# Branch A's last pair woven into the first gate product of a hybrid encoder layer, on one Trainium2 core

## The reference

```python
h = layer_norm(x, ln_in_g, ln_in_b)
proj = h @ w_in[l]
(aq, ak, av, ag, bq, bk, bv, bf, bg, cq, cg, mg) = split_columns(proj)
oa = swa_sink_attention(...)    # A: 16 query heads, 2 kv heads, window of 128, sinks, relative bias
ob = forgetting_attention(...)  # B: 16 heads, causal, cumulative forget bias
oc = memory_attention(...)      # C: 4 heads over 256 memory tokens
branches = (oa * silu(ag), ob * silu(bg), oc * silu(cg))
for n in range(3):
    gate = sigmoid(mg[..., n * D_MODEL:(n + 1) * D_MODEL] + b_gate[l, n])
    merged += gate * (branches[n] @ w_branch[l, n])
y = merged @ w_out[l]
h = layer_norm(alpha * h + y, ln_g[l], ln_b[l])
```

## Time and profile before

| | us |
|---|---|
| median of three runs | 1889.51 (1888.16 to 1889.75) |
| the profiled execution | 1889.29 |
| its span | 1887.7 |
| PE busy | 1852.6 (98% of the span) |
| DVE busy | 1221.1 (65%) |
| ACT busy | 829.6 (44%) |
| POOL busy | 162.1 (9%) |

### The profile page before, as it was taken

One profiled execution on the slowest core, in us unless ns is written; L12 is line 12 of the kernel. 1 busy time (PEld: TensorE's weight loads), 2 busy tenths in 40 slices (PEclk: granted clock), 3 DMA queues, 4 the chain that ended last, 5 costly groups with the idle time before them and its releaser, 6 DMA issues.

```text
span 1887.7 us, 24332 instructions
## 1 busy us (share of the span) xinstructions
PE 1852.6 (98%) x8599; PEld 1529.5 (81%) x8599; DVE 1221.1 (65%) x1909; ACT 829.6 (44%) x1360; POOL 162.1 (9%) x225
## 2 busy tenths in 40 slices
PE   8999999999999999999989999999999999999996
PEld 6888887888888888888878888888888888888884
DVE  5754335654555554677868878778788655576776
ACT  4652222544444444344445545455456333234543
POOL 1100000000000000000000000000001000002223
PEclk9999999999999999999999999999999999999998
DMA  8554446433333333333242623605437544439998
GB/s 306 189 153 127 128 134 205 117 86 96 102 91 91 88 90 95 98 98 103 85 162 71 212 85 139 223 23 200 144 124 247 200 155 145 147 115 242 242 210 193
DMA packets 227033, 271.95 MB, mean 144 GB/s; under 512 B 12768, under 2 KB 150032, under 8 KB 224784
## 3 DMA queue, kind: packets, MB, share of 16 engines
q1 hardware_dynamic: 196400, 188.24, 32.0%
q0 software_dynamic: 30416, 82.22, 16.3%
q10 hardware_dynamic: 144, 0.52, 0.1%
HBM read 229.38 MB, written 37.32 MB: 141 GB/s over the span
## 4 chain that ended last, share of the span: by engine, by line
PE 95%; DMA 2%; DVE 1%; POOL 1%; ACT 0%; issue 0%; DVEq 0%; POOLq 0%; SPq 0%; ACTq 0%
PE acc L634 13%; PE acc L636 13%; PE acc L635 13%; PE scores L958 4%; PE scores L956 4%; PE scores L954 4%; PE acc L954 3%; PE acc L958 3%; PE acc L956 3%; PE transposed L661 3%; PE scores L1024 2%; PE scores L1026 2%; PE scores L1025 2%; PE acc L1024 2%; PE acc L1026 2%; PE acc L1025 2%
## 5 line engine op out<-in xcount | busy, mean ns | idle before, releaser
L634 PE MATMUL acc<-h_hi,w_lo 128*128 128x512 f32 x1056 | 420.6, 398 | 0.0
L636 PE MATMUL acc<-h_hi,w_hi 128*128 128x512 f32 x1056 | 412.0, 390 | 0.0
L635 PE MATMUL acc<-h_lo,w_hi 128*128 128x512 f32 x1056 | 411.1, 389 | 0.0
L1557 DVE TENSOR_TENSOR w_lo<-raw_weights,w_hi 128x1024 fp32r<-128x1024 f32 x214 | 260.9, 1222 | 229.5 <-ACT w_hi L1106 224.0
L1106 ACT ACTIVATE w_hi<-raw_weights 128x1024 fp32r<-128x1024 f32 x214 | 225.8, 1058 | 277.9 <-PE acc L636 115.7
L1356 ACT ACTIVATE piece_split<-w 128x512 fp32r<-128x512 f32 x336 | 212.0, 632 | 221.5 <-PE acc L958 81.3
L2004 DVE TENSOR_TENSOR piece_split<-w,piece_split 128x512 fp32r<-128x512 f32 x336 | 231.9, 691 | 87.4 <-ACT piece_split L1356 78.5
L636 PEld LDWEIGHTS acc<-h_hi,w_hi 128*128 128x128 f32 x1056 | 198.2, 188 | 42.3
L634 PEld LDWEIGHTS acc<-h_hi,w_lo 128*128 128x128 f32 x1056 | 198.9, 188 | 41.1 <-issue 2.8
L635 PEld LDWEIGHTS acc<-h_lo,w_hi 128*128 128x128 f32 x1056 | 198.6, 188 | 39.7 <-issue 1.0
L954 PE MATMUL scores<-piece_split,h_sums 128*128 128x512 f32 x216 | 84.0, 389 | 0.0
(11 more groups left out here) (423 smaller groups left out, 3522.9 us busy)
## 6 DMA issues: line engine op xcount, KB each, us to landing
raw_weights<-in_w_in SPq DMA_DIRECT2D x134, 512.0 KB, 3.8
w<-in_w_in SPq DMA_DIRECT2D x96, 512.0 KB, 8.2
raw_weights<-in_w_branch SPq DMA_DIRECT2D x48, 512.0 KB, 5.2
raw_weights<-in_w_mem_kv SPq DMA_DIRECT2D x32, 512.0 KB, 5.2
gate<-gate_scratch POOLq DMA_DIRECT2D x12, 1024.0 KB, 6.6
gate_scratch<-first_product POOLq DMA_DIRECT2D x12, 512.0 KB, 6.7
out_w_x<-in_w_out POOLq DMA_DIRECT2D x12, 512.0 KB, 8.2
x_rows<-in_x SPq DMA_DIRECT2D x4, 1024.0 KB, 9.0
```

Of the source, the lines that this page charges most:

```text
L634: pe.matmul(bank_out, wl, hi[:, k, :], start=first, stop=False)
L635: pe.matmul(bank_out, wh, lo[:, k, :], start=False, stop=False)
L636: return pe.matmul(bank_out, wh, hi[:, k, :], start=False, stop=last)
L1557: dve.tensor_tensor(w_lo[:, slot, :], raw[:, slot, :], w_hi[:, slot, :].bitcast(F32), ALU.subtract).then_inc(lo_ready, 1)
```

## The change

1. **PE's order.** Of the last pair only turns 0 and 1 stay ahead of the gates. `gate_product` takes hooks: behind G1's piece 0 come turns 2 and 3, behind piece 1 the values stage.
2. **ACT and DVE.** Pieces 0 and 1 are split at the end of the last pass, ahead of the last tanh and silu, and so are turned tiles 0 and 1; tiles 2 and 3 follow the silu. `a_parts` stands behind piece 3. `a_gate` is cut into `a_join` (behind pieces 5 and 6) and `a_multiply` (behind piece 7).
3. **Banks.** In even groups G1 accumulates in `sc[0]`, `sc[1]` and G5 in `acc[0]`, `acc[1]`; in odd groups the third role changes likewise. G1 of the first group waits for the maxima of all scores (`a_negmax`), G5 for `acc_free`.
4. **Weight sums of the first group.** `first_sums` puts the first sums of pieces 0 to 3 behind the splits of pieces 4 to 7, and so on; the split of the tile `s3` (`h_lo`, second half of tokens) moves from G6 to G2.
5. **Loads.** `w_12` is loaded quarter by quarter, each as soon as the chunk that used its slot has been multiplied.
6. **Layout.** Branch A's probabilities and bias move down and its values and silu up, so that slots 0 and 1 of `p_split` are free in the last pass. The constants shrink by 160 bytes, and all of the region `R2` starts 160 bytes lower.

```diff
-    R2 = CONST + 3072
+    R2 = CONST + 2912
...
-                if g == 0:
-                    sp.wait_ge(multiplied, CH_M)
-                for d in range(4):
+                for n in range(CH_M - RING, CH_M):
+                    d = n % RING
                     if g:
                         sp.wait_ge(pc_lo, piece(g - 1, G7, 2 * d + 1) + 1)
+                    else:
+                        sp.wait_ge(multiplied, n + 1)
                     load_pieces(g, "12", w_12, 0, 1, d)
...
-            for t in range(TT):
-                a_turn_stage(PAIRS, t)
-            a_values_stage(PAIRS, 1)
-
+            a_turn_stage(PAIRS, 0)
+            a_turn_stage(PAIRS, 1)
+            a_end = {0: lambda: (a_turn_stage(PAIRS, 2), a_turn_stage(PAIRS, 3)),
+                     1: lambda: a_values_stage(PAIRS, 1)}
...
                     last.then_inc(pc_mult, 1)
+                    if between and k in between:
+                        between[k]()
...
-                a, b, c = (acc[0], acc[1]), (sc[0], sc[1]), (sc[2], ob)
+                a, b, c = (sc[0], sc[1]), (acc[0], acc[1]), (sc[2], ob)
                 z, y, x = (a, b, c) if g % 2 == 0 else (c, b, a)
+
+                if g == 0:
+                    pe.wait_ge(a_negmax, 2 * PAIRS)
+                else:
+                    pe.wait_ge(ev_c11, 2 * g)
+                gate_product(g, G1, z, True, False, a_end if g == 0 else None)
...
                     split_hi(CH_A + s, 4, i)
+                if at_end:
+                    at_end()
                 job_done(CH_A + 3, 4, i)
                 act.wait_ge(gated, 2 * BT + i)
                 tanh_half(JOB_A + 1, a_e[:, :])
...
-            piece_hi(0, G1, 0)
-            a_probs_hi(PAIRS, (0, 1, 2, 3))
-            act.wait_ge(a_o, PAIRS)
-            piece_hi(0, G1, 1)
-            a_parts(PAIRS)
+            def first_pieces():
+                piece_hi(0, G1, 0)
+                piece_hi(0, G1, 1)
+                a_probs_hi(PAIRS, (0, 1))
...
+            a_pass(PAIRS - 1, False, first_pieces)
+
+            a_probs_hi(PAIRS, (2, 3))
...
+                        if g == 0 and p == G1 and k == 3:
+                            a_parts(PAIRS)
...
                 a_normalise(i, steps)
+                if at_end:
+                    at_end()
                 silu(JOB_A + 1, 2, i, a_e[:, :], a_sg[:, :], 2 * HC + PAIRS + 1 + i, steps)
...
-            piece_lo(0, G1, 0)
-            a_probs_lo(PAIRS, (0, 1, 2, 3))
-            piece_lo(0, G1, 1)
-            a_gate(PAIRS)
-            dve.wait_ge(gated, 3 * BT)
+            def first_pieces():
+                piece_lo(0, G1, 0)
+                piece_lo(0, G1, 1)
+                a_probs_lo(PAIRS, (0, 1))
...
+            a_pass(PAIRS - 1, False, first_pieces)
             dve.sem_inc(ev_c12, 2)
-            dve.sem_inc(ev_c21, 2)
+            a_probs_lo(PAIRS, (2, 3))
...
+            first_sums = {at_pk: due for at_pk, due in sums_in.items() if at_pk[0] not in (G1, G5, G6)}
+            for k in range(4):
+                first_sums[G1, k + 4], first_sums[G5, k] = (1, k), (1, k + 4)
+                first_sums[G5, k + 4], first_sums[G6, k] = (2, k), (2, k + 4)
+                first_sums[G6, k + 4] = (3, k)
...
-                        if (p, k) in sums_in:
-                            weight_sum(g, *sums_in[p, k])
-                        if g == 0 and p == G6 and k == 4:
+                        if g == 0 and p == G1 and k in (5, 6):
+                            a_join(PAIRS, k - 5)
+                        if g == 0 and p == G1 and k == 7:
+                            a_multiply(PAIRS)
+                            dve.wait_ge(gated, 3 * BT)
+                            dve.sem_inc(ev_c21, 2)
+                        if (p, k) in (sums_in if g else first_sums):
+                            weight_sum(g, *(sums_in if g else first_sums)[p, k])
+                        if g == 0 and p == G2 and k == 2:
                             dve.wait_ge(s3_hi, 1)
```

More of the change, by code:

```diff
@@ L280, in program @@
     a_k = at(R2 + 2048, "a_k", [P, 2, SEQ], F32)
[L281 to L289, removed]
+    a_v = at(R2 + 16384, "a_v_hi_lo", [P, TT, 2, 2, 64], F32R)
+    a_sg = at(R2 + 20480, "a_silu", [P, SEQ], F32)
+    a_e = at(R2 + 22528, "a_tanh", [P, SEQ], F32)
+    a_bias = at(R2 + 6144, "a_bias", [P, 2, WIN], F32)
+    a_p = at(R2 + 8192, "a_probs", [P, TT, 2, 2 * P], F32)
+    a_sum = at(R2 + 24576, "a_attended", [P, TT, P], F32)
+    a_vt = at(R2 + 26624, "a_v_transposed", [P, SEQ], F32)
+    a_out = at(R2 + 26624, "a_gated", [P, SEQ], F32)
+    s3_buf = at(R2 + 28672, "s3_tile", [P, HALF], F32)
     a_pth = at(BR_HI, "a_probs_t_hi", [P, TT, 3 * P], F32R)
@@ L944, in _, with gate_product @@
                 left[p] = [h_sum[:, n, v, :, :] for v in range(2)]
-            def gate_product(g, p, banks, first, stop):
+            def gate_product(g, p, banks, first, stop, between=None):
                 hi, lo = left[p]
@@ L1303, in a_parts, with a_pass @@
                         .then_inc(a_part_ready, 1)
-            def a_pass(i, first):
+            def a_pass(i, first, at_end=None):
                 for s in range(4):
@@ L1867, in a_probs_lo, with a_join, a_multiply @@
                                       ALU.subtract).then_inc(copied, 1)
-            def a_gate(i):
-                for b in range(2):
-                    dve.wait_ge(a_part_ready, b + 1 - 2 + 2 * i)
-                    high = (ob, sc[2])[b][0:64, :].rearrange("p (t h q) -> p t h q", t=2, h=2)
-                    low = a_part[:, b, :].rearrange("p (t h q) -> p t h q", t=2, h=2)
-                    for hh in range(2):
-                        dve.tensor_tensor(a_sum[hh * 64:(hh + 1) * 64, 2 * b:2 * b + 2, :], high[:, :, hh, :],
-                                          low[:, :, hh, :], ALU.add).then_inc(a_summed, 1)
+            def a_join(i, b):
+                dve.wait_ge(a_part_ready, b + 1 - 2 + 2 * i)
+                high = (ob, sc[2])[b][0:64, :].rearrange("p (t h q) -> p t h q", t=2, h=2)
+                low = a_part[:, b, :].rearrange("p (t h q) -> p t h q", t=2, h=2)
+                for hh in range(2):
+                    dve.tensor_tensor(a_sum[hh * 64:(hh + 1) * 64, 2 * b:2 * b + 2, :], high[:, :, hh, :],
+                                      low[:, :, hh, :], ALU.add).then_inc(a_summed, 1)
+            def a_multiply(i):
                 dve.wait_ge(a_summed, 4 * i)
@@ L1983, in a_pass @@
                     if s == 1 and not first:
-                        a_gate(i)
+                        a_join(i, 0)
+                        a_join(i, 1)
+                        a_multiply(i)
                     if s == 2:
@@ L2040, in branch_lo @@
                                   ALU.subtract).then_inc(branch_ready, 1)
[L2042 to L2046 removed]
+            def first_pieces():
+                piece_lo(0, G1, 0)
+                piece_lo(0, G1, 1)
+                a_probs_lo(PAIRS, (0, 1))
+            dve.wait_ge(br_stored, 16 * (HC + PAIRS))
+            dve.wait_ge(toep_stored, 16 * PAIRS)
+            a_pass(0, True)
+            with dve.Fori(1, PAIRS - 1) as i:
+                a_pass(i, False)
+            a_pass(PAIRS - 1, False, first_pieces)
             dve.sem_inc(ev_c12, 2)
[L2048 removed]
+            a_probs_lo(PAIRS, (2, 3))
             sums_in = {(G6, 0): (2, BT - 1)}
```

22 lines of the change are left out of this document (6 added, 16 removed).

## The result

| | before | after |
|---|---|---|
| median, us | 1889.51 (1888.16 to 1889.75) | 1897.47 (1896.43 to 1899.22) |
| profiled execution | 1889.29 | 1896.43 |
| its span | 1887.7 | 1894.8 |
| PE busy | 1852.6 | 1866.3 |

A forecast was written before the change was run, and what follows sets the result against it. TensorE, busy 98% of the span, was taken as the bound. The stretch before G5 could give 9.6 us, less 1.8 and 0.2, stated as 7.5: 1889.5 - 7.5 = 1882.0 us, range 1880.0 to 1885.2.

The forecast's parts named there:

- the seam: Behind branch A's last pass, from the last pair's first transposes to G5: 23.66 us before, 7.5 us to be gained.
- its ceiling: Most that stretch before G5 could give with PE unstalled at full clock: 23.66 - 14.03 = 9.6 us.
- the first rival (half clock): Clock falls anyway between the last transposes and G5, slowing transposes, values and three pieces: 1885.0 us, chance 0.10.
- a free and of a longer DVE chain: DVE's chain in G1: no waits at pieces 6, 7, G5, 1879.9, chance 0.08; values later, 1884 to 1886, 0.10.
- the three that were named: PE waits on DVE's splits at G1's pieces 6 and 7 and G5's piece 0: 0.3 + 0.7 + 0.8 = 1.8 us.
- 9.6 less 1.8 and 0.2: Gain before G5: 9.6 us at most, less 1.8 of waits on DVE and 0.2 before values; stated as 7.5.
- part 5: Layout: second region's tiles start 160 bytes lower, read by 2016 gate matmuls; priced at nothing, tail 1 us either way.
- Slower: New offset slows gate matmuls' read of split pieces: gain gone from 3.7 ns each, 1895.9 us at 3%; chance 0.05.
- the tail: Accumulating DMAs from the last sums at the kernel's end, 11.60 and 5.10 us: 1 us either way in the range.
- Part 3, late sums: First group's weight sums four pieces behind the split: 1.8 us out of DVE's queue in G1, else piece 7 later.
- Part 4, loads: Last w_12 quarter, loaded from the last chunk's end, lands at 981 to 986; first sum delayed 0 to 1, taken as nothing.
- The rival of a load 4 us late: w_12 quarter lands at 989, 4 us after the first sum's turn: 1885.7 to 1889.5 us; chance 0.07 for any such wait.

The follow-up runs named there:

- before_at_256: The kernel before the change with only R2 moved from CONST + 3072 to CONST + 2944, a multiple of 256: 1904.49 us (one run).

## Why the prediction was wrong, point by point

**What was right.** The bound, the seam and its ceiling. Forecast for the seam was 16.1 us, measured 16.14; G5 was forecast at 992.6 and started at 992.63. Step by step: values wanted at 980.8, started at 980.83; the copies of the attended halves forecast for 982.6, at 982.65; piece 4's copy 983.55, at 983.63. The granted clock was 1.00 throughout, so the first rival (half clock) fell, and so did those of a free and of a longer DVE chain. The waits are the three that were named, on DVE at pieces 6 and 7 and at G5's first: 0.23 + 0.6 + 0.7 = 1.5 us in the starts (the first too short for the view of waits), against 1.8. Part of the difference is PE's own slower pieces (48 at 6.7 ns are 0.3 us), which ate into the waits: that is why the seam is as long in the changed kernel (16.14) as at distance 0 (16.13), and why the layout's loss begins only at G5. That gain and forecast agree to 0.02 us is partly luck: the old order's seam varies by more than 1 us from kernel to kernel, and the prediction's own terms, 9.6 less 1.8 and 0.2, make 7.6 and not 7.5.

**What was wrong: part 5.** "No row has a tile at the new offset, so the trace gives no price; I take nothing". The price was 13.2 us in the gates alone, more than the 7.5 us that the seam brought. The rival *Slower* had the place (the gate matmuls' read of split pieces), the point from which it decides (3.7 ns each) and the right sort of size ("at 3% it is 13.9 us lost"; measured 3.0%, 6.7 ns), and then was given 0.05, because nothing in the trace spoke for it. But its own next words were that nothing in the trace could speak against it. An unpriced term that multiplies 2016 instances of the bounding engine's instruction needs less than 2% to cancel the whole gain; with such a lever the absence of evidence deserved a far larger share, and a range that reached it. The rule of bounding an unseen cost from both sides was applied to the tail, "1 us either way", and not to the matmuls.

The mechanism was also not quite as the rival had it. It spoke of the new offset. The offset alone is harmless (1882.80 with the pieces at just that place); the distance to the tiles that the weights come from is what counts. A look at the layout could have suggested such a thing: before, every pair of operands of every large product lay a multiple of 256 bytes apart, so the trace had one case only.

**Output product.** Two of the four slots of its ring lie in `R2`. Its pace rose from 226.9 to 231.2 ns (means of the intervals below 0.3 us), 2.8 us over its 662 such intervals; the sum had no term for it. As a stage it became only 1.6 us longer, since the stalls in it were 1.3 us shorter in that execution. The stage by itself proves little: in the six other kernels at distance 0 it took 156.81 to 159.35 us.

**The tail.** By the prediction's estimate from the Trainium skill (DMA: Bandwidth & Descriptors, section How a descriptor splits into AXI transactions) the two accumulating DMAs would take 0.7 us longer from their new start, which lies further off a 256-byte boundary. The chain's tail shows none of it, 11.27 and 5.11 us against 11.60 and 5.10. The longer one took 10.67 to 11.60 us in the six kernels in which it keeps its old start, and 11.72 in before_at_256, where it starts at a multiple of 256; so a few tenths could hide in its spread, but no run speaks for them:

```profile
1847.85 11.27 DMA resid<-out_third_sum
...
1859.66 5.11 DMA resid<-out_second_quarter
```

**Part 3, late sums.** "With the old order piece 7 would be later by as much" as 1.8 us: measured 0.0. The step that failed is the accounting of DVE's queue: it was taken as one unbroken chain from the start, while ahead of piece 4's split stood 2.33 us of idle time in which the early sums fit. The seam's total was not touched by it, since the change does have the sums late.

**Part 4, loads.** "Between nothing and 1 us, I take nothing" held for the last quarter: the first sum at 984.89 followed its split without a wait. What I did not work out is what the quarters are worth, 4.0 us. The rival of a load 4 us late priced the same thing from the other side ("all but 3.8 us or less"), and the run with the undivided load gave it.

**The whole, with the distance mended.** 1889.5 - 7.5 = 1882.0 was the sum; the two versions at distance 0 measured 1883.84 and 1882.80, inside the range of 1880.0 to 1885.2, and by their ratios 5.9 and 7.0 us below the kernel before. The changed kernel lies 13.6 and 14.7 us above them. The edits of the change that concern order and loads were worth about what the sum said; one number of its layout cost nearly twice that.

## What to carry to other kernels

Before a tile that feeds the bounding engine is moved, look at the distance between the two operands of each of its products, and keep it a multiple of 256 bytes unless a run has priced another one (shown here for 512-column float32 products in an unbroken stream); a region that starts 160 bytes lower can cost more than an interleaving brings. When a kernel is slower without a wait and at the same clock, count instructions started in a window of equal length, since a duration of 394 instead of 389 ns does not catch the eye. A term for which the trace has no row is not zero: multiply it by the number of instances, and let the product decide how much chance it gets.

## What the runs showed of the hardware that was not expected

- The pace of back-to-back 512-column float32 matmuls depends on where their moving operands and weights start relative to each other: 226.7 ns at a distance of 0 modulo 256 bytes, 228.9 to 234.3 at the seven others tried, in steps of 32. In the kernel with both kinds of distance it changes one matmul ahead of the border and eight behind it. It is not a matter of the clock (1.00 in all windows of the gates) nor of the operands' own starts (0.0 us of difference in the gates when all is moved by 32).
- The granted clock fell to half behind waits of 2.71 us (before) and 2.38 us (with spare matmuls ahead), but not behind one of 2.39 us (before). In before_at_256 the eight transposes behind the same 2.71 us wait took 1.09 us, still at the full clock, and the clock fell in the values stage behind a wait of 1.17 us (0.84 from 982 to 983 us, 0.50 from 983 to 986). In the run with the undivided load it fell only at the fifth matmul after a wait of 3.42 us had ended:

```profile
991.57 0.50 PE L955 MATMUL scores<-piece_split,h_lo 128*128 128x512 f32 x1 [3.42 <-DVE piece_split L2012]
991.91 0.40 PE L957 MATMUL scores<-piece_split,h_hi 128*128 128x512 f32 x1
...
992.96 0.63 PE L959 MATMUL scores<-piece_split,h_hi 128*128 128x512 f32 x1
```

The length of the last wait alone does not tell when the clock falls; no run here shows what else enters.
